# 100 tokens gathered and 156 dense, instead of 96 and 160, in the expert layer of a transformer block on Trainium2

## What is computed

```python
qr = (hb @ w_pq).reshape(b, t, 8, 2, 128)
sc = jnp.einsum('bthpd,hpnd->bthpn', qr, sub_keys)
...
expert = i0 * 128 + i1                 # 16384 experts; 8 heads x 16 picks = 128 per token
g = jax.nn.softmax(c_top, axis=-1)
u = u_tab[expert]
a = gelu(einsum('bthkd,btd->bthk', u, hb))
return einsum('bthk,bthkd->btd', g * a, v_tab[expert])
```

## Time and profile before

| | |
|---|---|
| median of 3 runs | 1666.11 us (1665.05 to 1666.53) |
| the profiled execution, its time | 1668.66 us |
| its span, first to last instruction | 1666.9 us |
| mean granted clock of TensorE | 0.998 |
| TensorE matmul busy | 1654.3 us (99%) |
| VectorE busy | 1019.7 us (61%) |
| GpSimd busy | 273.2 us (16%) |
| moved by DMA | 569.90 MB, mean 342 GB/s |

### The profile page before, as it was taken

The page is one execution under the profiler, slowest core; times in us unless marked ns, Lnnn a source line. Parts: engine busy times, 40 slices in busy tenths (PEclk is TensorE's granted clock), DMA queues, the critical chain, the costliest instruction groups (busy, mean ns, idle before and its releaser), DMA issues.

```text
span 1666.9 us, 28850 instructions
## 1 busy us (share of the span) xinstructions
PE 1654.3 (99%) x11438; PEld 1569.3 (94%) x11438; DVE 1019.7 (61%) x1709; ACT 503.4 (30%) x1347; POOL 273.2 (16%) x252
## 2 busy tenths in 40 slices
PE   8999999999999999999999999999999999999999
PEld 6768888888999999999999999999999999999998
DVE  5426695767878999767777767753334333443333
ACT  6547567756551000035444454410000000000000
POOL 1020000000003222312222122121121212211110
PEclk9999999999999999999999999999999999999999
DMA  9764446466648999999999999999999999999996
GB/s 342 240 143 132 140 129 200 139 226 204 227 153 342 421 396 423 417 380 419 404 422 413 422 409 422 422 422 421 421 421 417 417 415 422 422 421 420 421 416 234
DMA packets 107057, 569.90 MB, mean 342 GB/s; under 512 B 11281, under 2 KB 13457, under 8 KB 48209
## 3 DMA queue, kind: packets, MB, share of 16 engines
q1 hardware_dynamic: 56768, 216.22, 35.0%
q0 software_dynamic: 31792, 220.50, 32.7%
q10 hardware_dynamic: 18432, 132.41, 19.3%
HBM read 563.04 MB, written 4.46 MB: 340 GB/s over the span
## 4 chain that ended last, share of the span: by engine, by line
PE 82%; DMA 12%; DVE 3%; issue 1%; ACT 1%; POOL 0%; ACTq 0%; DVEq 0%
PE ps L1586 33%; PE ps L1531 22%; PE ps L1318 5%; PE ps L1323 5%; PE ps L1320 5%; DMA acts<-in_u_rows,sel 5%; DMA late<-in_u_rows,sel 3%; DMA sel<-sel 2%; PE ps L1340 2%; PE ps L1482 2%; PE ps L1478 2%; PE ps L1477 2%; DVE w_lo L821 1%; DMA raw<-in_w_in 1%; PE ps L1548 1%
## 5 line engine op out<-in xcount | busy, mean ns | idle before, releaser
L1145 DVE SCALAR_TENSOR_TENSOR acts<-late,sel,acts 128x2048 f32<-128x2048 f32 x77 | 181.1, 2352 | 247.3 <-DMA late<-in_v_tab,sel 247.0
L1531 PE MATMUL ps<-acts,late 128*128 128x160 f32 x2048 | 287.9, 300 | 0.0
L1531 PE MATMUL ps<-acts,raw 128*128 128x160 f32 x2048 | 287.6, 300 | 0.0
L1586 PE MATMUL ps<-acts,raw 128*128 (+1 forms) x2048 | 283.8, 299 | 0.9 <-DMA raw<-in_v_tab 0.8
L1586 PE MATMUL ps<-acts,late 128*128 (+1 forms) x2048 | 284.2, 299 | 0.0
L1586 PEld LDWEIGHTS ps<-acts,raw 128*128 128x128 f32 x2048 | 279.8, 190 | 1.7 <-issue 1.7
L1531 PEld LDWEIGHTS ps<-acts,late 128*128 128x128 f32 x2048 | 280.5, 190 | 0.1
L1531 PEld LDWEIGHTS ps<-acts,raw 128*128 128x128 f32 x2048 | 280.4, 190 | 0.0
L1586 PEld LDWEIGHTS ps<-acts,late 128*128 128x128 f32 x2048 | 280.1, 190 | 0.1
L821 DVE TENSOR_TENSOR w_lo<-raw,w_hi 128x512 fp32r<-128x512 f32 (+1 forms) x288 | 188.8, 682 | 131.6 <-ACT w_hi L544 129.4
L544 ACT ACTIVATE w_hi<-raw 128x512 fp32r<-128x512 f32 (+1 forms) x288 | 170.3, 622 | 86.9 <-PE ps L1482 41.9
(11 more groups left out here) (224 smaller groups left out, 1526.0 us busy)
## 6 DMA issues: line engine op xcount, KB each, us to landing
raw<-in_w_in SPq DMA_DIRECT2D x72, 512.0 KB, 3.7
raw<-in_u_tab SPq DMA_DIRECT2D x33, 1024.0 KB, 9.6
late<-in_u_tab SPq DMA_DIRECT2D x33, 1024.0 KB, 9.6
raw<-in_v_tab SPq DMA_DIRECT2D x32, 1024.0 KB, 9.9
raw<-in_v_tab ACTq DMA_DIRECT2D x32, 1024.0 KB, 9.9
late<-in_v_tab SPq DMA_DIRECT2D x32, 1024.0 KB, 10.0
late<-in_v_tab ACTq DMA_DIRECT2D x32, 1024.0 KB, 9.9
raw<-in_u_tab ACTq DMA_DIRECT2D x31, 1024.0 KB, 9.5
```

Source lines behind the costliest of these rows:

```text
L1145: V.scalar_tensor_tensor(acc, row[n % NROW], w_sp[:, n - N_OWN:n - N_OWN + 1], acc, ALU.mult, ALU.add).then_inc(row_used, 1)
L1531: ins = mm(ps[:, q, 0:N_DN], ring[q][:, k * P:k * P + P], hF[:, k, :], start=k == 0, stop=k == KD - 1)
L1586: ins = mm(ps[:, pair_bank(k // 2), at:at + N_DN], ring[q][:, k * P:k * P + P], acts[:, ds(i * (4 * N_DN) + q * N_DN, N_DN)], start=first ...
```

## The change

100 tokens are gathered and 156 are dense. Partitions 0 to 99 own a token each, partitions 100 to 124 are 25 helpers, and 125 to 127 do nothing in the gathered part. A helper takes 24 picks from each of four tokens, 96 in all, so each owner keeps 104: there are 104 gathers per table, the first 96 on 125 partitions and the last 8 on 100. The dense products have 156 columns, and there are 39 gate groups; the first gated chunk is still 48. VectorE takes 17 rows in 16 chunks where it took 15. The helpers' picks are copied in two DMAs of 8 where there was one of 16, their vectors and sums in four parts where there were three. The last sums of the helpers leave 8 rows before the end.

```diff
@@ sizes (L67 to L76) @@
-    SHARE = 4
-    N_SP = P - P // SHARE
+    N_SP, N_HELP, N_SLOT, N_TURN = 100, 25, 4, 24
...
-    N_OWN = N_PICK * N_SP // P
-    N_TURN = N_PICK - N_OWN
+    N_OWN = N_PICK - N_TURN
+    N_LENT = N_SLOT * N_TURN
     N_GRP = N_DN // 4
-    FIRST_G = NKEY - 2 * N_GRP
+    FIRST_G = NKEY - 2 * N_GRP - 2
...
-        lenders, helpers = [slice(i, P, SHARE) for i in range(SHARE - 1)], slice(SHARE - 1, P, SHARE)
+        lenders, helpers = [slice(N_HELP * i, N_HELP * i + N_HELP) for i in range(N_SLOT)], slice(N_SP, N_SP + N_HELP)
+        owners, others, workers = slice(0, N_SP), slice(N_SP, P), slice(0, N_SP + N_HELP)
@@ SyncE, the rows of the output (L420) @@
             sp.wait_ge(acc_sum, 1)
-            for rows in lenders:
-                sp.dma_start(io["out"][rows, :], acc[rows, :]).then_inc(out_sent, 16)
+            sp.dma_start(io["out"][owners, :], acc[owners, :]).then_inc(out_sent, 16)
@@ GpSimd, gather and lend_picks (L471 to L496) @@
-                pool.indirect_dma_start(row[n % NROW], None, table, bass.IndirectOffsetOnAxis(ap=idx[:, k:k + 1], axis=0)).then_inc(row_in[n % NROW], 16)
+                parts = workers if k < N_LENT else owners
+                pool.indirect_dma_start(row[n % NROW][parts, :], None, table, bass.IndirectOffsetOnAxis(ap=idx[parts, k:k + 1], axis=0)).then_inc(row_in[n % NROW], 16)
...
                 pool.wait_ge(idx_ready, N_AHEAD + h)
-                at = N_OWN + TOPK * (h % 2)
-                pool.dma_start(idx[helpers, TOPK * h:TOPK * h + TOPK], idx[lenders[h // 2], at:at + TOPK]).then_inc(idx_in, 16)
-                pool.wait_ge(idx_in, 16 * (h + 1))
+                for at in range(TOPK * h, TOPK * h + TOPK, 8):
+                    rows, src = lenders[at // N_TURN], N_OWN + at % N_TURN
+                    pool.dma_start(idx[helpers, at:at + 8], idx[rows, src:src + 8]).then_inc(idx_in, 16)
+                pool.wait_ge(idx_in, 32 * (h + 1))
@@ GpSimd, the order of its work (L512 to L524) @@
             gathers(NROW + 24, N_TURN + 2 * NROW)
+            pool.wait_ge(row_used, N_TURN)
+            pool.dma_start(hs[0][helpers, :], hs[0][lenders[2], :]).then_inc(hs_in, 16)
+            gathers(N_TURN + 2 * NROW, N_TURN + 3 * NROW)
             pool.wait_ge(gsp_ready, 1)
             for i, rows in enumerate(lenders):
                 pool.dma_start(w_sp[helpers, N_TURN * i:N_TURN * i + N_TURN], w_sp[rows, N_OWN:N_PICK]).then_inc(gsp_in, 16)
-            pool.wait_ge(row_used, N_TURN)
-            pool.dma_start(hs[0][helpers, :], hs[0][lenders[2], :]).then_inc(hs_in, 16)
-            gathers(N_TURN + 2 * NROW, N_OWN + N_TURN + 2 * NROW)
-            for i in range(2):
+            gathers(N_TURN + 3 * NROW, 2 * N_TURN + 2 * NROW)
+            pool.wait_ge(row_used, 2 * N_TURN)
+            pool.dma_start(hs[1][helpers, :], hs[1][lenders[3], :]).then_inc(hs_in, 16)
+            gathers(2 * N_TURN + 2 * NROW, N_OWN + N_TURN + 2 * NROW)
+            for i in range(N_SLOT):
                 pool.wait_ge(turn_kept, i + 1)
                 pool.dma_start(lent[lenders[i], :], acc_copy[helpers, :]).then_inc(lent_in, 16)
...
-            pool.wait_ge(row_used, 2 * N_OWN)
-            pool.dma_start(lent[lenders[2], :], acc[helpers, :]).then_inc(lent_in, 16)
@@ VectorE, next_row (L1133) @@
-                        V.scalar_tensor_tensor(row[n % NROW], row[n % NROW], 1.0, hs[turn % 2], ALU.mult, ALU.mult,
-                                               accum_out=a_sel[:, n:n + 1]).then_inc(row_used, 1)
+                        V.scalar_tensor_tensor(row[n % NROW][workers, :], row[n % NROW][workers, :], 1.0, hs[turn % 2][workers, :], ALU.mult, ALU.mult,
+                                               accum_out=a_sel[workers, n:n + 1]).then_inc(row_used, 1)
@@ VectorE, the gated chunks (L1233 to L1257) @@
             hots(0)
-            hots(1)
             apply(FIRST_G)
             apply(FIRST_G + 1)
             next_row()
-            gate(0)
-            hots(2)
+            hots(1)
             apply(FIRST_G + 2)
             next_row()
-            gate(1)
-            g = 2
+            gate(0)
+            g = 1
...
-                if rows_done[0] < N_OWN and c % 16 != 15:
-                    next_row()
+                if rows_done[0] < N_OWN:
+                    next_row(2 if c % 16 == 0 else 1)
@@ VectorE, the end of the gathered rows (L1269) @@
-            for turn in range(3):
+            dve.wait_ge(unit_used, NKEY)
+            for turn in range(N_SLOT):
                 next_row(N_OWN + (turn + 1) * N_TURN - rows_done[0])
-                if turn < 2:
...
+            next_row(2 * N_OWN - rows_done[0])
+            dve.wait_ge(row_used, 2 * N_OWN)
+            dve.wait_ge(lent_in, 16 * N_SLOT)
             V.tensor_tensor(acc, acc, lent, ALU.add).then_inc(acc_sum, 1)
@@ TensorE (L1556) @@
             for q in range(4):
                 u_chunk(FG, q)
-                if q >= 2:
-                    gate_group(q - 2, q - 2, True)
-            with pe.Fori(FG + 1, NKEY // 4) as i:
+            gate_group(0, 0, True)
+            for q in range(4):
+                u_chunk(FG + 1, q)
+                if q % 2 == 0:
+                    gate_group(1 + q // 2, 1 - q // 2, q == 0)
+            with pe.Fori(FG + 2, NKEY // 4) as i:
```

More of the change, by code:

```diff
@@ L411, in _ @@
             sp.wait_ge(x2_stored, 16)
[L412 removed]
+            sp.wait_ge(unit_used, NKEY + X_CHUNKS)
             for n in range(8):
@@ L415, in _ @@
                 cols = slice(512 * (n // 2), 512 * (n // 2) + 512)
-                rows = helpers if n % 2 else slice(P, SEQ)
+                rows = others if n % 2 else slice(P, SEQ)
                 sp.dma_start(x_rest[n % 2][:, cols], io["x2_scratch"][rows, cols]).then_inc(x2_back, 16)
@@ L426, in _ @@
                 sp.dma_start(io["out"][P:SEQ, cols], o_rest[0][:, cols]).then_inc(out_sent, 16)
-                sp.dma_start(io["out"][helpers, cols], o_rest[1][:, cols]).then_inc(out_sent, 16)
-            sp.wait_ge(out_sent, 16 * (8 + SHARE - 1))
+                sp.dma_start(io["out"][others, cols], o_rest[1][:, cols]).then_inc(out_sent, 16)
+            sp.wait_ge(out_sent, 16 * 9)
             sp.wait_ge(x2_stored, 16)
```

68 lines of the change are left out of this document (31 added, 37 removed).

## The result

The changed kernel takes **2579.57 us** (median of 4 runs, 2571.32 to 2585.82), the kernel before 1666.32 us beside it. The ratio is 1.5476, with a 95% interval from 1.542 to 1.5531. Forecast were 1668 us, and 1700 at most.

The account below looks back on a forecast made before the run. TensorE and DMA were both taken as at their limit, with bytes deciding: 28 us less on TensorE, 19.9 us more bytes; the steps ended at 1668.3 us, 1.4 over the span, forecast 1668, range 1650 to 1700.

Parts of the forecast that it names:

- the price of gathers of 125 and 100 rows: In both tables' gathers: they cost by their bytes, as gathers of 128 rows do, 19.9 us at 421 GB/s.
- Rival B: Gathers of 125 and 100 rows load the DMA engines unevenly, slower: 1683 us in the mild form; chance 0.25.
- its hard form: Gathers fall on few engines; a tenth of the gathers' part unused gives 129 us more, 1795 us; chance 0.12.
- Bytes: Gathers of both tables: 12800 rows per table instead of 12288, 8.4 MB more in all, 19.9 us slower.
- Columns: Dense products on TensorE: four columns fewer save 3.3 ns each, 27.3 us together in the two stages.
- rival D: Dense products are held by their weights, so fewer columns buy nothing: median about 1673 us; chance 0.05.
- step 2: Gated chunks up to the last row of `u_tab`: 149.1 MB at 414 GB/s, 360 us, last row at 1076.
- step 4: V stage: 244.1 MB at 418 to 421 GB/s, 584 to 580 us, last gathered row at 1658.
- Rival C: Pauses at the copies of the picks grow: three more of 5 us each with the DMA idle, 1683; chance 0.05.
- step 5: Behind the last row: its sum, the helpers' sum and nine output DMAs, 10.3 us, to 1668.3.
- step 3: Seven chunks to the end of the u stage: 31 us, to 1107, where it was 1101.
- landing times of 30 us and more: Sign for the gathers: such times, or a DMA share well under 1 while VectorE waits, would show rival B.

Follow-up runs that it names:

- run 2: Changed kernel with every gather made full, on all 128 partitions, the extra rows fetched and not used: 1714.14 us, ratio 1.0281 to the kernel before.
- run 3: Kernel before with gathers and VectorE's and ScalarE's work on them on partitions 0 to 124 only: 2513.86 us, ratio 1.5075.
- run 1: Gathers of random 8 KB rows alone, five in flight, then one at a time: 128 rows 411 GB/s, every other count 200 to 237.
- Run 6: Gathers alone, five in flight, only destination partitions differing: 64 rows on 0 to 63 194 GB/s, every second partition 350 with start and end, 0 to 31 187.
- run 10: Changed kernel with 100 full gathers of 128 rows per table instead of 104, some picks left out: 1707.56 us, ratio 1.0236 to the kernel before.
- run 11: The kernel with 100 full gathers per table, copies of the picks for gathers 32, 48, 64 and 80 issued 8 gathers earlier: 1699.39 us, ratio 1.0192.
- run 9: Changed kernel with its 125-row gathers made full, the last 8 of each table left at 100 rows: 1758.58 us, ratio 1.0547 to the kernel before.

## Why the prediction was wrong

- **The step that failed** is the price of gathers of 125 and 100 rows: "I take the lower, since the trace has only full ones and the bytes explain every stage of it." Bytes explained every stage because every gather was full; that was no evidence for one that isn't. Runs 2 and 3 show this step from both sides: full gathers in the changed kernel take it from 2580 to 1714 us, 125 rows in the kernel before take it from 1668 to 2514. In its place the runs showed 4.2 us for an average gather of the changed kernel above a full one, (2580 - 1714) / 208, where the sum had nothing, and a rate of 227 to 245 GB/s for all transfers where it had 414 to 421.
- **Rival B had the right place and the wrong size.** That 125 rows fall on 5 engines is borne out by the count of small packets. But its hard form ended at 1795 us, by two assumptions that failed. "As long as five gathers in flight cover all 16 engines, nothing is lost": the share was 0.98 to 1.02 all the time, and the rate half. And it charged the gathers alone; the units lost as much, 20 us to land instead of 10. A rate of 421/16 GB/s was written to the engines, and an engine does move 27 where a gather goes alone (run 1). But the runs with 8 and 4 ports show about the same rate as a limit of a port, which the trace could not tell apart since its rows lay across all 128 partitions; with five gathers of 125 rows in flight an engine moves 211/16 = 13 GB/s. The Trainium skill's rule on the number of engines is right and would not have given the time either, as 112 rows show.
- **A rule was read past.** The Trainium skill, page "SBUF — State Buffer", section "Door 1: The DMA port swizzle", measures a transfer of 1 MiB to 0 to 63 at 196 GB/s and one to 0 to 31 at 189. Run 6 agrees, with 194 and 187. The forecast asked how many engines a gather uses and never how many ports it reaches. Even so, that section alone gives 100 and 125 rows all 16 ports: it would have named the resource, not the loss.
- **The sign** was right, in part by luck. Of the 0.56 for slower 0.25 was rival B, which had the place; the rest, and the 1668 itself, came from rows that had nothing to do with the cause. The range should have reached far up, since the price of the one new operation had no row at all and its upper end was argued, not bounded.
- **Bytes** were right: 8.4 MB forecast for a full-rate case, 8.44 in run 10.
- **Columns**: in the v stage's line on `late` a product took 296 ns in runs 2 and 10, 299 before, the 3.3 ns forecast. In the u line it is 299 to 300 as before over the whole stage, at a granted clock of 0.96 to 0.97 in the gated part; before that part, from 516 to 712 us of run 10, it is 296 on `late` and 299 on `raw`. So rival D fell in the v stage.
- **Steps 2 and 4** were too fast by themselves. Had the gathers been full, the forecast would have missed by 40 us (run 10). It used 414 and 418 to 421 GB/s, rates of stages in which TensorE never paused. Once rows hold back `apply` and `gelu`, TensorE pauses, the units behind it are not asked for, and the DMA too falls idle, as in the stretch with 243 GB/s. That is 404 instead of 414 in the gated part. In the v stage the share stayed at 1.01, so idle engines don't explain its 413, and that stays open. Rival C saw the pauses at the picks, worth 8 of these 40 us by run 11. The end shows where the sum came out short. In the profiled execution of run 10 the last row that VectorE had to wait for landed at 1676.6 us, 19 us after the forecast's 1658. Behind it VectorE had five rows and a return of helper sums still to do, without a pause; the last four:

  ```profile
  1681.60 9.72 DVE L1145 SCALAR_TENSOR_TENSOR acts<-late,sel,acts 125x2048 f32<-125x2048 f32 x4
  ```

  The span ended at 1703.8, 27 us after that landing, where step 5 had 10.3 with one row in it: 17 us more.
- **The full-gather run's 1714** met its expectation of 1715 by chance. The 248 MB of that sum already hold what the seven chunks of step 3 move, yet 1715 comes out only with their 31 us added once more: by the prediction's own steps it is 716 + 368 + 590 + 10 = 1684 us, and the run was 30 us slower, as run 10 was 40.
- **What would show it**: "landing times of 30 us and more" came true (61.5 us); "DMA share well under 1" did not, and by that sign alone B would have been ruled out. GpSimd waited for VectorE's buffers in the v stage, as was said (602.5 us). TensorE was idle too, though not before `u_chunk` for `gelu`, as was said, but at the gate products and for its units.

**What the mechanism is, and what stays open.** Where the rows lie evenly over the ports a gather reaches, a port carries about 26.5 GB/s (424/16, 207/8, 110/4), and what seems to count is how many ports the engines write at a time. The Trainium skill, page "DMA: Bandwidth & Descriptors", section "The descriptor swizzle", has it that in a transfer to 128 partitions each engine gets the eight of one port, partitions p to p+3 and p+32 to p+35; no view here shows which engine takes which row. Such a dealing keeps sixteen engines on sixteen ports. If 120 rows are dealt in blocks of 8 neighbours instead, engines 32 partitions apart meet at one port, 8 ports work at a time, and the rate is 212 GB/s; measured were 229 with 120 rows and 227 with 112. This reading for 125, 120, 112, 100 and 96 rows was argued, not shown: by reach alone 120 rows could have 397 GB/s. Run 1 speaks against its simplest form, in which the engines of one gather meet: one gather of 112 rows alone had 284 and 295 GB/s in two stretches of 2.5 us at a share of 0.92 and 0.91, above the 212, and one of 125 rows alone lost nothing per row. At least part of the loss needs several gathers in flight. The reading also doesn't say why 64 rows on the even partitions escape it, 413 GB/s in the steady part of run 6.

## What to carry to other kernels

Gather on all 128 partitions, even if the last rows are thrown away: 28 rows fetched for nothing are 0.23 MB, 0.5 us at 421 GB/s; leaving them out cost 3.3 us each time (run 9). When a change gives a DMA a shape that the trace has never shown, time that shape by itself, in a kernel of a few lines, before the sum is made, and with as many in flight as the kernel has: one at a time 112 rows cost 6.2 us against 5.6 (run 1), and the halved rate doesn't show. A DMA share of 1.0 says that the engines are occupied, not that they move what they can: read it beside the GB/s.

## What the runs showed of the hardware

Where a gather reaches 4, 8 or 16 ports evenly, its rate goes by them: 103 to 110, 180 to 209 and 404 to 431 GB/s in their steady parts, for 16 to 128 rows of 8 to 32 KB. Gathers of 96 to 125 neighbouring rows, five in flight, reach all 16 and still get 200 to 237; one of 125 alone uses five engines at 27 GB/s each. A gather at half rate slows the full transfers beside it: units of 1 MB landed in 20 us instead of 10. Splitting a gather costs little if both parts reach all ports: 192 more gathers took some 10 us, 0.05 us each. And a stall on the DMA spreads to TensorE's clock: a mean of 0.80 in the stages with 37% idle time, where it had been 1.00.
